# Two transformer blocks on one core: the join from the last convolved down product to the pooling mixer and the next feed-forward, rearranged by token halves

## The chip, the cores and the metric

The kernel runs on one NeuronCore of a Trainium2 chip. The metric is the device time of one execution, in microseconds (us). All five engines of the core are used: TensorE (PE, matrix products into PSUM), VectorE (DVE), ScalarE (ACT), GpSimd (POOL), and SyncE (SP), which issues the DMA transfers of the weights.

## The reference

Two blocks are computed one behind the other, in float32, on 512 tokens of width 1024. The change lies in the second. Its input is 16 meta tokens and 512 tokens (528 in all); its layers alternate a mixer and a convolved feed-forward:

```python
def pool_mixer(h, w_group, scale):
    hf = h.astype(jnp.float32).reshape(B, L, N_POOL_GROUPS, POOL_GROUP_DIM)
    csum = jnp.cumsum(hf, axis=1)
    for g, w in enumerate(POOL_WINDOWS):          # 2, 4, 8, 16
        cg = csum[:, :, g, :]
        prev = jnp.pad(cg[:, :L - w], ((0, 0), (w, 0), (0, 0)))
        means.append((cg - prev) / jnp.minimum(t, float(w))[None, :, None])
    mixed = (jnp.stack(means, axis=2) - hf)
    return jnp.einsum('blgc,gcd->blgd', mixed, w_group).reshape(B, L, D) * scale

def conv_ffn(h, w_up, conv_w, conv_b, w_down):
    u = conv_b + sum(conv_w[j] * up[:, j:j + L] for j in range(CONV_WIDTH))   # up = padded h @ w_up
    gate, val = jnp.split(u, 2, axis=-1)
    return (jax.nn.silu(gate) * val) @ w_down

for i in range(2):                                # mixer 0 is attention, mixer 1 is pooling
    h = h + rmsnorm(mixer_i(rmsnorm(h, norm_mix_pre[i])), norm_mix_post[i])
    f = conv_ffn(rmsnorm(h, norm_ffn_pre[i]), ...)
    h = h + rmsnorm(f, norm_ffn_post[i])
```

## The kernel before

Activations are stored transposed: a tile holds 128 channels on the partitions and the tokens along the columns, so X, the residual stream, is 8 tiles (KD = 8) of 528 columns (S2; S3 = 516 columns from the second feed-forward on, since the first tokens are no longer needed there). Every product is made exact enough by splitting both factors into a high and a low part of type fp32r: three products high*high, high*low, low*high (lines 642, 644, 646). A *unit* is one block of weights that fills a slot: its raw values come by DMA (a ring of 4), ScalarE makes the high part (`act_hi`, line 582), GpSimd the low part (`pool_unit`, line 567), TensorE uses it (`pe_unit`). 528 columns do not fit one PSUM bank, so a unit writes a *pair* of banks, PS[0] to PS[3], half of the columns in each. Each engine has its own program, written out by hand in the order in which it is to run, and semaphores join them.

The norm is put behind the product: a tile is multiplied by its gain and split (`act_split`, `dve_split`, line 745), and the product is scaled by 1/rms when it leaves PSUM. The sum of squares comes from ScalarE's squares (`act_square`, line 740) by either VectorE adding them (`dve_acc`, line 755) and one product with a matrix of ones (`pe_norm`, line 658), or by eight products with ones that add up in PSUM (`pe_square`, line 665). Then come the mean (`dve_norm`, line 794), exp(-0.5 ln) on ScalarE (lines 775, 776) and a Newton step on VectorE (`newton`, lines 780 to 782).

The stretch that is changed runs like this in the kernel before:

1. the last down product of the first convolved feed-forward (`cffn0`, 8 units of 6 row tiles, in a run-time loop), each unit over all 528 columns; VectorE adds each unit to M (line 1241), ScalarE squares it, VectorE adds the square to `acc`;
2. `pe_post`, `dve_post`, `act_post`: the norm of M, then for each of 8 tiles a scaled copy (line 1264) and the addition to X (line 1268); ScalarE splits and squares the new X; TensorE sums these squares;
3. `dve_pool`, `pe_pool`, `act_pool`: the pooling product comes before the pooling (the two commute), 4 units for 4 groups (line 2979); ScalarE takes it out of PSUM with the pool scale into `grouped` (line 2991); VectorE multiplies it by 1/rms into `pa` (line 3036), makes the window sums by doubling spans (`window_sums`, line 3037: 1, 2, 3 and 4 additions over two tiles at once), corrects the first 16 columns (line 3041) and writes the mixed tile to M (line 3043), which ScalarE squares and TensorE sums;
4. `dve_post` again, and the first unit of `cffn1` (`pe_first_unit`), its row tiles interleaved with the sums of the squares of the new X.

An earlier join, from attention to `cffn0` (`act_mla_out`, `dve_mla_out`, `pe_skewed`), already works by halves of 264 columns. The gate path's forward scans (line 1745) are VectorE's only `tensor_tensor_scan`.

## Time and profile before

| | |
|---|---|
| median of 3 runs | 2317.04 us (2314.05 to 2332.53) |
| the profiled execution | 2314.94 us, of which the span is 2313.1 us |
| TensorE busy | 2244.0 us, 97% of the span |
| VectorE, ScalarE, GpSimd busy | 48%, 38%, 43% |
| mean granted TensorE clock | 0.988 |

The profiled execution lies 2.1 us under the median of the three runs. Times in the rows are microseconds from the start of the span unless they are marked ns. "Idle before" names the time in which the engine did nothing ahead of an instruction, and whose work ended that. The granted clock is given as a share of full speed, 2.4 GHz; 0.5 is 1.2 GHz. Operations that follow each other on an engine overlap by some tenths of a microsecond, so a chain of them is read from the distance of their starts.

### The profile page before, as it was taken

Reading aid. Unit: us, or ns where it says so; the run is one execution under the profiler, and the core shown is the slowest. Engines: PE = TensorE matmul, PEld = TensorE weight load, DVE = VectorE, ACT = ScalarE, POOL = GpSimd, SP = SyncE. Lnnn points to the kernel's source line nnn. Section 1 sums busy time; section 2 is a strip of 40 time slices with the busy share of each in tenths; the row PEclk is TensorE's granted clock in tenths of the full one; section 3 lists DMA queues with packets and bytes.
Section 4 is the critical chain, followed back from the end, with each engine's and each line's share of the span. In section 5 each row is a group of like instructions: output and inputs, shape, how many; then the busy total and the mean of one; then the engine's idle time right before and its main releaser. Section 6 shows DMA issues by size and latency. Waiting matters only on the chain.

```text
span 2313.1 us, 34738 instructions
## 1 busy us (share of the span) xinstructions
PE 2244.0 (97%) x13485; PEld 1953.1 (84%) x13485; DVE 1112.8 (48%) x1639; ACT 878.9 (38%) x1674; POOL 987.1 (43%) x747
## 2 busy tenths in 40 slices
PE   8999999999999999999999999999999868999998
PEld 6888887778887788888797879999999848989897
DVE  5313235637634532232476655752625487626255
ACT  4323234432443422222454446432423344424244
POOL 3545454542472454544451124244444412444443
PEclk9999999999999999999999999999999979999999
DMA  5333333331351233333220113133332211233332
GB/s 159 91 95 96 94 91 99 87 87 46 94 162 56 82 92 99 91 97 94 85 70 26 34 38 101 38 91 92 91 92 84 72 37 56 91 101 91 92 92 73
DMA packets 336226, 194.06 MB, mean 84 GB/s; under 512 B 7357, under 2 KB 327506, under 8 KB 336098
## 3 DMA queue, kind: packets, MB, share of 16 engines
q1 hardware_dynamic: 335570, 191.13, 28.4%
q8 instruction: 85, 1.39, 0.2%
q10 hardware_dynamic: 528, 1.19, 0.2%
q14 instruction: 43, 0.35, 0.0%
HBM read 190.20 MB, written 2.10 MB: 83 GB/s over the span
## 4 chain that ended last, share of the span: by engine, by line
PE 90%; DVE 6%; ACT 2%; issue 1%; POOL 1%; DMA 0%; DVEq 0%; POOLq 0%; SPq 0%; ACTq 0%
PE PS L642 23%; PE PS L646 23%; PE PS L644 23%; PE PS L2545 2%; PE PS L2563 2%; PE PS L949 2%; PE PS L950 2%; PE PS L951 2%; PE PS L2599 1%; PE PS L2617 1%; PE PS L665 1%; PE PS L1601 1%; PE PS L1602 1%; PE PS L1603 1%; PE PS L1945 1%
## 5 line engine op out<-in xcount | busy, mean ns | idle before, releaser
L567 POOL TENSOR_TENSOR w_lo<-raw,w_hi 128x512 fp32r<-128x512 f32 (+5 forms) x711 | 944.4, 1351 | 1270.7 <-ACT w_hi L582 1270.6
L582 ACT ACTIVATE w_hi<-raw 128x512 fp32r<-128x512 f32 (+5 forms) x711 | 395.9, 605 | 790.9 <-PE PS L646 682.2
L642 PE MATMUL PS<-XHI,w_hi 128*128 128x264 f32 (+2 forms) x2056 | 539.0, 320 | 16.1 <-DVE XLO L745 13.8
L644 PE MATMUL PS<-XLO,w_hi 128*128 128x264 f32 (+2 forms) x2056 | 531.9, 316 | 0.0
L646 PE MATMUL PS<-XHI,w_lo 128*128 128x264 f32 (+2 forms) x2056 | 530.8, 316 | 0.0
L642 PEld LDWEIGHTS PS<-XHI,w_hi 128*128 128x128 f32 x2056 | 340.4, 189 | 49.7 <-issue 18.2
L646 PEld LDWEIGHTS PS<-XHI,w_lo 128*128 128x128 f32 x2056 | 339.8, 189 | 25.2
L644 PEld LDWEIGHTS PS<-XLO,w_hi 128*128 128x128 f32 x2056 | 339.4, 189 | 25.6 <-issue 1.0
L642 PE MATMUL PS<-h_hi,w_hi 128*128 128x512 f32 (+1 forms) x704 | 210.1, 339 | 1.7 <-DVE h_lo L1218 1.6
L644 PE MATMUL PS<-h_lo,w_hi 128*128 128x512 f32 (+1 forms) x704 | 210.4, 340 | 0.0
L646 PE MATMUL PS<-h_hi,w_lo 128*128 128x512 f32 (+1 forms) x704 | 210.3, 339 | 0.0
L1185 DVE TENSOR_TENSOR u_buf<-PS,rn 128x512 f32<-128x512 f32 (+2 forms) x88 | 61.3, 696 | 233.4 <-PE PS L646 233.4
L646 PE MATMUL PS<-x_hi,w_lo 128*128 128x512 f32 x352 | 139.4, 396 | 0.0
L644 PE MATMUL PS<-x_lo,w_hi 128*128 128x512 f32 x352 | 139.2, 395 | 0.0
L642 PE MATMUL PS<-x_hi,w_hi 128*128 128x512 f32 x352 | 139.1, 395 | 0.0
L642 PEld LDWEIGHTS PS<-h_hi,w_hi 128*128 128x128 f32 x704 | 120.9, 188 | 18.6 <-DVE h_lo L1218 1.6
L646 PEld LDWEIGHTS PS<-h_hi,w_lo 128*128 128x128 f32 x704 | 120.8, 188 | 15.2
L644 PEld LDWEIGHTS PS<-h_lo,w_hi 128*128 128x128 f32 x704 | 120.4, 188 | 15.4
L1121 ACT ACTIVATE h_hi<-hid 128x512 fp32r<-128x512 f32 (+5 forms) x88 | 56.0, 637 | 200.7 <-DVE hid L1216 200.5
L1185 DVE TENSOR_TENSOR g_buf<-PS,rn 128x512 f32<-128x512 f32 (+2 forms) x88 | 61.0, 693 | 97.1 <-PE PS L646 96.9
L1237 DVE SCALAR_TENSOR_TENSOR X<-PS,X 128x512 f32<-128x512 f32 x48 | 33.2, 691 | 148.5 <-PE PS L646 148.5
L1218 DVE TENSOR_TENSOR h_lo<-hid,h_hi 128x512 f32 (+5 forms) x88 | 69.6, 790 | 72.3 <-ACT h_hi L1121 72.3
(409 smaller groups left out, 3382.9 us busy)
## 6 DMA issues: line engine op xcount, KB each, us to landing
raw<-in_ffn_w_up SPq DMA_DIRECT2D x132, 512.0 KB, 3.8
raw<-in_ffn_w_down SPq DMA_DIRECT2D x70, 512.0 KB, 3.8
raw<-in_ffn_w_gate SPq DMA_DIRECT2D x44, 512.0 KB, 3.8
raw<-in_w_in SPq DMA_DIRECT2D x25, 512.0 KB, 3.8
raw<-in_ffn_w_down SPq DMA_DIRECT2D x24, 384.0 KB, 3.4
raw<-in_xattn_w_kv SPq DMA_DIRECT2D x16, 512.0 KB, 3.9
raw<-in_w_out SPq DMA_DIRECT2D x8, 512.0 KB, 3.9
raw<-in_xattn_w_q SPq DMA_DIRECT2D x8, 512.0 KB, 4.1
```

The lines of the kernel that those rows point to most:

```text
L567: ins = nc.gpsimd.tensor_tensor(d, r, h.bitcast(F32), ALU.subtract)
L582: ins = nc.scalar.activation(d, r, ACT.Copy)
L642: nc.tensor.matmul(ps, wh, ahi(k)[:, c:c + w], start=(k == 0), stop=False)
L644: nc.tensor.matmul(ps, wh, alo(k)[:, c:c + w], start=False, stop=False)
L646: ins = nc.tensor.matmul(ps, wl, ahi(k)[:, c:c + w], start=False, stop=(k == u.kt - 1))
L949: nc.tensor.matmul(ps, h_hi[:, k, ts], s_hi[:, cs], start=start, stop=False)
L950: nc.tensor.matmul(ps, h_hi[:, k, ts], s_lo[:, cs], start=False, stop=False)
L951: return nc.tensor.matmul(ps, h_lo[:, k, ts], s_hi[:, cs], start=False, stop=stop)
L1121: nc.scalar.activation(h_hi[:, a + 2 * it, 0:w], hid[:, 0:w], ACT.Copy).then_inc(hid_hi, 1)
L1185: nc.vector.tensor_tensor(sv(dst, blk), psv(m % 4, blk), r, ALU.mult).then_inc(unit_read, 1)
L1218: nc.vector.tensor_tensor(h_lo[:, a + 2 * it, 0:w], hid[:, 0:w], h_hi[:, a + 2 * it, 0:w].bitcast(F32), ALU.subtract).then_inc(hid_lo, 1)
L2545: ins = nc.tensor.matmul(bank[:, 0:CW], w, x[:, k, c * CW:(c + 1) * CW], start=st, stop=sp_)
```

## The change

All of it lies between the last down product of `cffn0` and the first up products of `cffn1`.

- The columns are cut in two halves, QA (270 tokens) and QB (258). The last down product runs its 8 units over QA first, then over QB. It is no longer a run-time loop. The first three units leave their last row tile for later, and 5 of 6 row tiles of unit 0 over QB run before it. Seven of the eight units' weights are held in slots of their own (`dx`, `dc`), since they are used twice; the eighth and the first two pool units use the usual slots.
- Norm, addition to X and split of half QA run on VectorE and ScalarE while TensorE works on QB of the down product. The pooling product also goes by halves: 8 products over QA, then 8 over QB, through six PSUM banks. Squares of the new X go to eight places for QA (in `ws`, `sq`) and five for QB, so that they need not wait for TensorE's sums.
- Pooling itself keeps the full width: `pa` is filled by halves (two tiles in one instruction), and the window sums of groups 1 to 3 are now two `tensor_tensor_scan` instructions per group (a running sum that adds the newest column and subtracts the one that leaves the window); group 0 keeps one addition.
- The low parts of the first two units of `cffn1` are made by VectorE (`dve_low`), not by GpSimd; these two and the next two have slots of their own.
- Behind the pooling sums TensorE issues 44 products of the identity with itself (`SPARE`), whose result nobody reads.
- The first two units of `cffn1` are summed together, row tile by row tile (`pe_join_up`), the squares of the new X go to four places, and a tile's low part is issued one step earlier than before (in iteration k for tile k - 2, was k - 3). The first up stage of `cffn1` is written out as that of `cffn0` is.

```diff
@@ -311,6 +318,13 @@
     M_tok = flat(M)[:, 0:NT * D].rearrange("p (t d) -> p t d", t=NT)
     e_hi, e_lo = ([flat(t)[:, i * SLOT:(i + 1) * SLOT] for i in range(2)] for t in (XHI, XLO))
     gain_row = flat(sq)[:, 0:D]
+    QA, QB = slice(0, QW[0]), slice(QW[0], S2)
+    SQM = [flat(sq)[:, i * QW[0]:(i + 1) * QW[0]] for i in range(2)]
+    ws_row = ws[:, :, :, :].rearrange("p a b s -> p (a b s)")
+    SQA = [ws_row[:, i * QW[0]:(i + 1) * QW[0]] for i in range(KD - 1)] + [SQM[0]]
+    SQC = [ws_row[:, i * S3:(i + 1) * S3] for i in range(4)]
+    SQB = [flat(sq)[:, 2 * QW[0]:2 * QW[0] + QW[1]], flat(sq)[:, 2 * QW[0] + QW[1]:2 * S2], acc[:, 0:QW[1]],
+           acc[:, QW[1]:2 * QW[1]], fin_rn[:, 0:QW[1]]]
 
     PS = [ctx.enter_context(nc.psum_tensor(f"PS{i}", [P, 2, 512], F32)) for i in range(4)]
 
...
+    N_DOWN, N_POOL, N_CF1 = PHASE["pool"] - KD, PHASE["pool"], PHASE["cffn1"]
+    held_of = lambda t, at: (t[:, at, 0, :], t[:, at, 1, :])
+    HELD.update({N_DOWN + i: held_of(dx, i) for i in range(5)})
+    HELD.update({N_DOWN + 5 + i: held_of(dc, i) for i in range(2)})
+    HELD.update({N_POOL + i: (w_hi[:, N_POOL % SPLIT, i * 512:(i + 1) * 512], w_lo[:, N_POOL % SPLIT, i * 512:(i + 1) * 512])
+                 for i in range(2)})
+    HELD.update({N_POOL + 2: held_of(dc, 1), N_POOL + 3: held_of(dc, 0)})
+    HELD.update({N_CF1 + i: (flat(x2_hi)[:, i * SLOT:(i + 1) * SLOT], flat(x2_lo)[:, i * SLOT:(i + 1) * SLOT])
+                 for i in range(4)})
+    assert (N_DOWN + 7) % SPLIT == (N_CF1 + 5) % SPLIT != N_POOL % SPLIT == (N_CF1 + 4) % SPLIT
+
...
+        def half(j, c, ks=None, ready=None):
+            return pe_unit(pe, n + j, 0, FLAT[n + j], lambda k: h_hi[:, k, :], lambda k: h_lo[:, k, :],
+                           [(bank(down_pair(j), c), QA.stop * c, QW[c])], ready, signal=False, wait=False, ks=ks)
...
+        for j in range(3):
+            pe.wait_ge(unit_read, n + j - 3)
+            half(j, 0, range(nt - 1), (lambda k: pe.wait_ge(hid_lo, h0 + k + 1)) if j == 0 else None)
+        half(0, 1, range(nt - 1))
+        pe.wait_ge(hid_lo, h0 + nt)
+        for j in range(3):
+            pe_q.inc(half(j, 0, range(nt - 1, nt)), ("a", j))
+        for j in range(3, KD):
+            if j == 3:
+                pe.wait_ge(unit_read, n)
+            else:
+                dve_q.wait(pe, ("ma", j - 4))
+            pe_q.inc(half(j, 0), ("a", j))
+        half(0, 1, range(nt - 1, nt)).then_inc(unit_summed, 1)
+        for j in range(1, KD):
+            if j >= 4:
+                pe.wait_ge(unit_read, n + j - 3)
+            half(j, 1, ready=sum_a if j == 1 else None).then_inc(unit_summed, 1)
+
...
+            product_a(m)
+        for k in range(6):
+            square_a(k)
+        pe.wait_ge(unit_read, N_DOWN + 7)
+        for g in range(3):
+            product_b(2 * g)
+            product_b(2 * g + 1)
+            square_b(2 * g)
+            square_b(2 * g + 1)
+            if g < 2:
+                square_a(6 + g)
+        square_b(6)
+        product_b(6)
+        square_b(7)
+        product_b(7)
+        evicted(pe, 14)
+        for k in ALL:
+            pe_square(pe, S_POOLP, 3, 2, k)
+        for _ in range(SPARE):
+            nc.tensor.matmul(PS[0][:, 1, 0:P], ident, ident, start=True, stop=True)
+
+    def pe_join_up(pe, n):
+
+        def part(j, ks):
+            return pe_unit(pe, n + j, 0, FLAT[n + j], lambda k: hi(k, 3), lambda k: lo(k, 3), outs_of((n + j) % 4, 3),
+                           signal=ks[-1] == KD - 1, wait=False, ks=ks)
+
         pe.wait_ge(unit_read, n)
-        for k in range(KD):
-            pe_square(pe, S_POOL, SUMS, 2, k)
-        for g in range(4):
-            pe.wait_ge(lo_done, 2 * (n + g + 1))
-            s = (n + g) % SPLIT
-            pe.wait_ge(x_lo, KD * D_POOL + 2 * g + 2)
-            for mt in range(2):
-                m = 2 * g + mt
-                if m >= 3:
-                    pool_out(pe, m - 3)
-                for k in range(2):
-                    c0 = k * 256 + mt * P
-                    wh, wl = w_hi[:, s, c0:c0 + P], w_lo[:, s, c0:c0 + P]
-                    for w, x, st, sp_ in ((wh, hi, k == 0, False), (wh, lo, False, False), (wl, hi, False, k == 1)):
-                        for ps, c, cw in outs_of(m % 3, 2):
-                            ins = nc.tensor.matmul(ps, w, x(2 * g + k, 2)[:, c:c + cw], start=st, stop=sp_)
-            ins.then_inc(unit_summed, 1)
-        pe.wait_ge(norm_ms, S_POOL + 1)
-        for m in range(KD):
-            pe_square(pe, S_POOLP, SUMS, 2, m)
...
+        square_a(3)
+        square_a(4)
+        post_b(2)
+        square_a(5)
+        evict(6)
+        post_b(3)
+        evict(7)
+        square_a(6)
+        post_b(4)
+        square_a(7)
+        post_b(5)
+        evict(8)
+        evict(9)
+        post_b(6)
+        evict(10)
+        evict(11)
+        post_b(7)
+        dve_q.wait(act, "mspa")
+        act_q.inc(act_rsqrt(act, sd[:, QA], ms[:, QA]), "sdpa")
+        act.wait_ge(norm_ms, S_POOL + 1)
+        act_rsqrt(act, sd[:, QB], ms[:, QB]).then_inc(norm_sd, 1)
+        evict(12)
+        evict(13)
+        evict(14)
+        evict(15)
+        for k in ALL:
+            dve_q.wait(act, ("xm", k))
+            act_square(act, S_POOLP, k, k, M[:, k, :], S2)
+            if k in (1, 3):
+                hi_at(N_CF1 + k // 2)
+        act_sqrt(act, S_POOLP, S2)
+
...
+        def pooled(g, win):
+            tiles, sums = (2 * g, 2 * g + 1), ws[:, g % 2]
+            if g == 0:
+                link(nc.vector.tensor_tensor(sums, pa[:, 0:2, 16:], pa[:, 0:2, 15:S2 + 15], ALU.add))
+            else:
+                for i, k in enumerate(tiles):
+                    link(nc.vector.tensor_tensor_scan(sums[:, i, :], pa[:, k, 16:], pa[:, k, 16 - win:S2 + 16 - win], 0.0,
+                                                      ALU.add, ALU.subtract))
             cor = const[:, C_COR + 16 * g:C_COR + 16 * (g + 1)]
             for i in range(2):
-                link(nc.vector.tensor_tensor(src[:, i, 16:32], src[:, i, 16:32], cor, ALU.mult))
+                link(nc.vector.tensor_tensor(sums[:, i, 0:16], sums[:, i, 0:16], cor, ALU.mult))
             for i, k in enumerate(tiles):
-                pool_mixed.inc(nc.vector.scalar_tensor_tensor(M[:, k, :], src[:, i, 16:], 1.0 / win, pa[:, k, 16:], ALU.mult,
-                                                              ALU.subtract), k)
-        pool_mixed.wait(dve, KD - 1)
+                dve_q.inc(nc.vector.scalar_tensor_tensor(M[:, k, :], sums[:, i, :], 1.0 / win, pa[:, k, 16:], ALU.mult,
...
+        link(nc.vector.memset(pa[:, :, 0:16], 0.0))
+        dve.wait_ge(norm_sd, S_CF0P + 1)
+        root(QB)
+        for k in range(KD + 2):
+            post_b(1, k, QB, G_FPOST[0], low_b)
+            if k == 8:
+                pe_q.wait(dve, ("sx", KD - 1))
+                dve_q.inc(mean(QA, bank(1, 0)), "mspa")
+        dve.wait_ge(acc_done, KD * (S_POOL + 1))
+        mean(QB, bank(1, 1)).then_inc(norm_ms, 1)
+        act_q.wait(dve, "sdpa")
+        root(QA)
+        for g in range(4):
+            normed(g, 0)
+        dve.wait_ge(norm_sd, S_POOL + 1)
+        root(QB)
+        for g, win in enumerate(WINDOWS):
+            normed(g, 1)
+            pooled(g, win)
+        dve.wait_ge(lo_done, 2 * N_CF1)
+        dve_low(dve, N_CF1, 0)
+        dve_low(dve, N_CF1, 1)
+        dve.wait_ge(acc_done, KD * (S_POOLP + 1))
+        nc.vector.tensor_scalar(two(ms[:, 0:S2]), psv(3, 2), 1.0 / D, EPS, ALU.mult, ALU.add).then_inc(norm_ms, 1)
+        dve_low(dve, N_CF1 + 1, 0)
+        dve_low(dve, N_CF1 + 1, 1)
+        dve.wait_ge(norm_sd, S_POOLP + 1)
+        root(slice(0, S2))
+        for k in range(KD + 2):
+            post_b(2, k, slice(0, S2), G_POST[1], lambda m: dve_split(dve, D_CF1, m, 3, G_FPRE[1]))
+        dve_norm(dve, link, S_CF1, (N_CF1 + 3) % 4, 3)
 
 
```

The halves' bodies on VectorE (`post_a`: scale, low part of the tile before, addition to X; `acc_a`, `acc_b`: add a square; `normed`: below) stand in this order in `dve_join`:

```diff
+        def normed(g, c):
+            q, at = (QA, QB)[c], 16 + c * QW[0]
+            for m in (2 * g, 2 * g + 1):
+                evicted(dve, c * KD + m)
+            link(nc.vector.tensor_tensor(pa[:, 2 * g:2 * g + 2, at:at + QW[c]], M[:, 2 * g:2 * g + 2, q],
+                                         rn[:, q].rearrange("p (o w) -> p o w", o=1).to_broadcast([P, 2, QW[c]]), ALU.mult))
+
...
+        act_q.wait(dve, "sda")
+        root(QA)
+        add_half(1, 1)
+        add_half(2, 1)
+        acc_b(0)
+        post_a(0)
+        post_a(1)
+        add_half(3, 1)
+        acc_b(1)
+        post_a(2)
+        post_a(3)
+        acc_b(2)
+        add_half(4, 1)
+        post_a(4)
+        acc_b(3)
+        post_a(5)
+        add_half(5, 1)
+        post_a(6)
+        acc_b(4)
+        add_half(6, 1)
+        acc_b(5)
+        add_half(7, 1)
+        acc_b(6)
+        post_a(7)
+        post_a(8)
+        dve.wait_ge(norm_sum, len([x for x in range(S_CF0P + 1) if x not in PE_SUMMED]))
+        mean(QB, PS[0][:, 0, 0:QW[1]]).then_inc(norm_ms, 1)
```

## Rows read from the trace of the kernel before

**Rows 1.** the page: the chain that ended last, by engine
```profile
PE 90%; DVE 6%; ACT 2%; issue 1%; POOL 1%; DMA 0%; DVEq 0%; POOLq 0%; SPq 0%; ACTq 0%
```

**Rows 2.** busy us and count of each engine, granted clock, DMA share, GB/s, by stretch
```profile
1810.00:1840.20 30.20, 29.51 (x240) 29.33 (x240) 10.56 (x16) 11.06 (x22) 16.05 (x14) 1.00 0.25 73
1840.20:1862.90 22.70, 12.19 (x38) 8.46 (x39) 17.34 (x26) 12.54 (x21) 1.40 (x2) 0.70 0.11 32
...
1870.00:1900.70 30.70, 15.65 (x70) 11.92 (x68) 29.79 (x34) 9.87 (x17) 7.39 (x6) 0.73 0.24 68
1900.70:1914.60 13.90, 3.90 (x9) 2.55 (x9) 8.32 (x13) 5.17 (x9) 0.00 (x0) 0.62 0.00 1
1914.60:1919.20 4.60, 4.60 (x18) 4.19 (x19) 4.60 (x8) 1.23 (x2) 0.00 (x0) 0.58 0.02 4
```

**Rows 3.** TensorE alone: busy us and count, granted clock, DMA share, GB/s
```profile
1852.00:1857.00 5.00, 4.72 (x11) 0.50 0.00 0
1857.00:1862.00 5.00, 4.99 (x20) 1.00 0.00 0
```

**Rows 4.** who TensorE waited for, 1780 to 1960 us: total, times, longest
```profile
PE PS L665 <- ACT sq L740: 22.6, 5, 7.9
PE PS L642 <- DVE XLO L745: 9.9, 1, 9.9
...
PE PS L642 <- DVE h_lo L1218: 0.9, 1, 0.9
```

**Rows 5.** timeline of VectorE: start, us, instruction, count [idle before it]
```profile
1870.00 2.29 DVE L3036 TENSOR_TENSOR pa<-grouped,rn 128x528 f32<-128x528 f32 x2
...
1873.65 2.37 DVE L3041 TENSOR_TENSOR pb<-pb,const 128x16 f32<-128x16 f32 x2
...
1877.30 3.47 DVE L3036 TENSOR_TENSOR pa<-grouped,rn 128x528 f32<-128x528 f32 x2
...
1892.21 1.44 DVE L3036 TENSOR_TENSOR pa<-grouped,rn 128x528 f32<-128x528 f32 x2
...
1899.36 1.33 DVE L3043 SCALAR_TENSOR_TENSOR M<-pc,pa 128x528 f32<-128x528 f32 x2
1904.79 0.71 DVE L794 TENSOR_SCALAR ms<-PS 128x528 f32<-128x528 f32 x1 [4.11 <-PE PS L665]
...
1913.69 0.75 DVE L745 SCALAR_TENSOR_TENSOR XLO<-X,cols,XHI 128x516 fp32r<-128x516 f32 x1
```

**Rows 6.** timeline of TensorE at the first unit behind pooling
```profile
1914.58 0.77 PE L642 MATMUL PS<-XHI,w_hi 128*128 128x258 f32 x2 [9.90 <-DVE XLO L745]
...
1920.38 1.03 PE L665 MATMUL PS<-sq,const 128*128 128x258 f32 x4
...
1921.97 1.03 PE L665 MATMUL PS<-sq,const 128*128 128x258 f32 x4
```

**Rows 7.** timeline of VectorE in the earlier join by halves (264 columns)
```profile
1431.42 0.43 DVE L2855 TENSOR_SCALAR ms<-PS 128x264 f32<-128x264 f32 x1 [1.05 <-PE PS L2455]
...
1434.21 0.43 DVE L2874 TENSOR_TENSOR post_t<-M,rn 128x264 f32<-128x264 f32 x1
...
1440.21 0.49 DVE L2877 SCALAR_TENSOR_TENSOR XLO<-X,cols,XHI 128x264 fp32r<-128x264 f32 x1
...
1441.65 0.42 DVE L2874 TENSOR_TENSOR post_t<-M,rn 128x264 f32<-128x264 f32 x1
```

**Rows 8.** the only scans: count, ns min/median/max, first and last start
```profile
L1745 DVE TENSOR_TENSOR_SCAN t<-const,t x4: 2130/2136/2203, 426.5 to 433.1; 128x512 f32<-128x512 f32 x4
```

**Rows 9.** VectorE, 1840 to 1935 us: busy us, mean ns, idle before
```profile
L3037 DVE TENSOR_TENSOR pb<-pa 128x1086 f32<-128x1086 f32 x4 | 5.2, 1290 | 0.1
```

**Rows 10.** timeline of ScalarE in the earlier join by halves
```profile
1438.00 0.52 ACT L2727 ACTIVATE XHI<-X,cols 128x264 fp32r<-128x264 f32 x1 [0.59 <-DVE X L2881]
...
1438.74 0.37 ACT L2722 ACTIVATE sq<-PS 128x264 f32<-128x264 f32 x1
```

**Rows 11.** GpSimd, 1803 to 1842 us: busy us, mean ns, idle before
```profile
L567 POOL TENSOR_TENSOR w_lo<-raw,w_hi 128x384 fp32r<-128x384 f32 x14 | 16.6, 1209 | 16.7 <-ACT w_hi L582 16.7
```

More of the change, by code:

```diff
@@ L400, in ffn_units @@
                     segs += [Unit(1, D, lambda i, k=f0 + j: row[k]) for j in range(n)]
+                continue
+            if straight_end and f0 + n == FT:
+                segs += [Unit(n, P, lambda i, j=j, dv=dv: dv[:, :, j, :]) for j in range(KD)]
                 continue
@@ L1112, in up @@
                         ahead(n, 2 * it + a, 2 if 2 * it + a < PAIRED else 1)
[L1113 removed]
+                    elif not third:
                         look(it, n, 2 * a + 1, count)
@@ L3045, in dve_pool @@
-        pool_mixed.wait(dve, KD - 1)
+                dve_q.inc(nc.vector.scalar_tensor_tensor(M[:, k, :], sums[:, i, :], 1.0 / win, pa[:, k, 16:], ALU.mult,
+                                                         ALU.subtract), ("xm", k))
+        add_half(0, 0)
+        for j in range(1, KD):
+            add_half(j, 0)
+            acc_a(j - 1)
+        acc_a(KD - 1)
+        add_half(0, 1)
+        pe_q.wait(dve, "sa")
+        dve_q.inc(mean(QA, bank(3, 0)), "msa")
+        act_q.wait(dve, "sda")
```

420 lines of the change are left out of this document (300 added, 120 removed).

## Prediction

> **What bounds the kernel now.** The chain of waits is 90% TensorE [rows 1], so nearly everywhere only fewer or faster products would help. The exception is the join that the change rewrites. The table of stretches [rows 2] cuts it up: in the last down product (1810 to 1840) TensorE is busy for 29.5 of 30.2 us, 0.123 us for each of 240 instructions; in the norm and split behind it (1840.2 to 1862.9) for 12.2 of 22.7; in pooling (1870.0 to 1900.7) for 15.7 of 30.7, while VectorE works for 29.8; in the last norm (1900.7 to 1914.6) for 3.9 of 13.9. The waits [rows 4] name the cause: 22.6 us for squares from ScalarE, themselves late by VectorE, and 9.9 us for the first low part. So between 1840 and 1915 VectorE's chain sets the end, and it is this chain that has to be priced. From 1914.6 on TensorE is the bound again; its start there is cold: clock 0.58 over 4.6 us [rows 2], against 1.59 us for one row tile with its square later on [rows 6]. Two row tiles that would take 3.2 us took 4.9 (1914.58 to 1919.47), so at full clock the same work would have started at 1914.58 + 1.7 = 1916.3. That is the time to beat.
>
> **1. Down product by halves.** 36 instructions of 264 columns for a unit become 18 of 270 and 18 of 258, the same columns. The wait for the last hidden tile (0.9 us, [rows 4]) goes, covered by five row tiles of unit 0's second half (5 x 3 x 0.123 = 1.8 us). But the weights are now wanted every 2.2 us in the first pass, where they were wanted every 4.4. GpSimd makes a unit's low part in 2 x 1.2 us [rows 11], slower than that; the slots of their own let it start early, and I charge 0.3 us. Gain 0.6: the product ends near 1839.5. Lower bound of the gain: each of the five last units late by 2.4 - 2.2 gives 1 us more.
>
> **2. To the second half's norm.** Half QA is complete 5 x 2.2 + 8.5 us after the start at 1803.7, near 1823.4, and its sum, queued in unit 1 of QB, near 1826.2. From mean to scaled first tile the earlier join takes 2.8 us [rows 7], so VectorE has the root at 1829.0. Until the last low part of QA it issues 8 x 3 instructions for the tiles, 7 additions of QB and 7 accumulations, 38 in all. The earlier join issues 4 in 1.44 us [rows 7], 0.36 each: 13.7 us; with waits for ScalarE's high parts I take 15, near 1844. The addition to M of unit 7 stands in that queue and comes at 1842, not at 1839.5, and the sum of QB's squares behind it, whose products on TensorE stand between pooling products 1 and 2. Mean, 2.8 us, and ScalarE's copies ahead of its root (1 us): root of QB near 1848. Before it was 1848.8. So the hidden work buys less than 1 us here: it moved in front of the end and then VectorE is late with the end.
>
> **3. To the sum of the new X's squares.** VectorE needs 8 x 3 x 0.36 = 9 us more. ScalarE must issue 19 instructions until the sixth QA square, at 0.37 each (two in 0.74, [rows 10]) some 6.5 us from 1846.4: 1852.9. Behind that square TensorE's queue holds 7 pooling products over QB (6 x 0.12 = 0.72 us each), 8 sums over QB and 2 over QA. A sum over all columns costs 1.59 - 0.73 = 0.87 us [rows 6], a half 0.43: together 5.0 + 4.3 = 9.4, with handoffs 10.3. The mean is made at 1863.2. If the clock fell, this block would double (rival C). VectorE then idles 3 us, since the root of QA is queued behind this wait.
>
> **4. To the start of the window sums.** Mean 0.47, two roots of 3 x 0.47, and four instructions that scale half QA over two tiles (540 elements, as long as one of 528: 0.72 + 0.03, [rows 5], two in 1.44): 0.47 + 2.8 + 3.0 = 6.3 us, 1869.5. Before: 1870.0 [rows 5]. So up to here 0.5 us.
>
> **5. Window sums.** Removed: 10 additions over two tiles, 1.29 us each [rows 9] and 0.03 between, of which one stays in group 0: 9 x 1.32 = 11.9 us. Added: 6 scans. The only scans of the trace take 2.14 us for 512 elements [rows 8], 4.2 ns for an element, while a two-input addition over 528 takes 0.72. For 528: 2.20 + 0.03, 6 of them 13.4 us. So the scans alone cost 1.5 us. The operations differ (multiply and add there, add and subtract here), so I keep bounds: nothing saved at 2.2, and 0.73 each (a plain addition) would give 9.0 us back. I take 2.2, the row of the instruction itself. The Trainium skill (DVE: opcode table, instruction layouts, handler registers and perf-mode slots; Datapath and trigger behaviour) says that the built-in scan "runs at half throughput". By that a scan would be an estimated 1.25 us and the sum 5.9 us lower; the trace does not agree, 2.14 us is about a quarter of an element per cycle.
> Half of the scaling is done ahead (4 x 0.75 = 3.0 us, charged in step 4). And GpSimd is silent now: before, it made low parts at 1870 to 1880, and the first two pairs of scalings took 2.29 and 3.47 us where the undisturbed pair at 1892.21 took 1.44 [rows 5]. The corrections of group 0 took 2.37 us; in group 3 they are 1899.36 - 1892.21 less the pair (1.48) and four additions (5.28), so 0.39. Together 0.85 + 2.03 + 1.98 = 4.9 us of the 30.7 were this disturbance. New length: group 0 0.75 + 1.33 + 0.41 + 1.25 = 3.7; each other group 0.75 + 4.46 + 0.41 + 1.25 = 6.9; sum 24.4 against 30.7, a gain of 6.3 (4.9 + 3.0 - 1.5). The pair of mixed tiles that ends it starts at 1892.6 (before 1899.36), the mean stays 5.4 us behind, since TensorE is still at 0.5 there: 1898.0 (before 1904.79). The four low parts on VectorE (0.7 us each) fit the idle 4.1 us before this mean and the 1.4 us of ScalarE's root; without that cover they would cost 2.8.
>
> **6. The first unit.** From the mean to the first low part was 8.9 us [rows 5]; it is issued one iteration earlier, two instructions of 0.65 less (two mixed tiles in 1.33, [rows 5]): 7.6, so TensorE could start at 1898.0 + 7.6 + 0.9 = 1906.5. But the 44 spare products are queued ahead. One is two instructions of 128 columns; a 258-column one takes 0.22 us, which bounds it below at 0.107, and the 0.123 of a 264-column fp32r instruction with its weight load is what I take: 88 x 0.12 = 10.6 us (9.4 at least). TensorE starts at 1908.6, 2 us after it could, but warm: it came up within 5 us of steady work at 1852 to 1857 [rows 3], and the two last sums (3.9 us) stand in front. I add 0.3 for a cold rest. 1908.9 stands against 1916.3. Summing two units together makes TensorE's work per row tile 0.73 + 0.73 + 0.87 = 2.33 us, above VectorE's three instructions (1.95), so nothing waits; the product work is the same, its norm comes 2 us later relative to the start and is wanted only after four units (30 us). Held slots and the written-out stage repeat `cffn0`, where TensorE shows no wait.
>
> **Sum.** 0.5 (steps 1 to 4) + 6.3 (5) + 1.3 - 2.1 + 1.7 - 0.3 (6) = 7.4 us. The profiled execution took 2314.94, giving 2307.5; the median before is 2.1 above that execution, and I put half of that on: 2308.5.
>
> **Rivals.** A, scans nearer to a plain addition (bound 0.73 us): up to 9 us more, 2299 to 2304. For it: other operations than in the row. Against: the feedback is the same. B, the spare products are slow, no gain at the end: should TensorE stay at 0.5 through them, each takes twice 0.107, and all 88 x 0.215 = 18.9 us, the first unit starts at 1898.0 + 18.9 = 1916.9 and runs warm later: 2315 to 2317, no change. Against it [rows 3]: steady work raised the clock in under 5 us. C, which ends slower: TensorE's work in the join is now cut in pieces with pauses, the clock falls at about 1848 and stays low, so the 10.3 us of step 3 become 20.6 and the mean comes at 1873.5. The start of pooling slips by as much, the end is 10.3 - 7.4 = 3 us slower, 2319 to 2320. It decides once more than 7 us of step 3's work runs at 0.5. For it: 0.5 in all of pooling's fragments; against: no pause here is over 2 us, and [rows 3]. D, more is gained in steps 2 to 4 than my queue count allows (ScalarE and VectorE never wait for each other, the mean at 1860): 2305. E, the front is not won: GpSimd late with the low parts and ScalarE at its full 0.52 us for an instruction put 3 to 4 us in front of step 4: 2311 to 2313.
>
> **Numbers.** Chances: forecast 0.50, A 0.13, B 0.08, C 0.07, D 0.08, E 0.14. The range 2301 to 2316 leaves out part of A and C, and the scatter of single runs. A measurement of this kernel tells about 1%, 23 us, from no change. All cases lie inside that: same 0.93, faster 0.04 (a scan as cheap as an addition and half of the whole join hidden too), slower 0.03 (C together with waits that I don't see).
>
> **What would show it.** Scans at 2.2 us for 528 (1.25 would be the page's, 0.7 A's); VectorE's mean before pooling near 1863 and `pa` from 1869.5; no scaling over 0.8 us; pooling 24 to 25 us long; mean behind it near 1898; spare products 10 to 11 us at clock 1.0; first unit of `cffn1` near 1909, its row tiles 2.33 us apart. Wrong would be: a clock of 0.5 between 1850 and 1863, TensorE waiting for low parts in the first pass over QA, or a new wait of TensorE in `cffn1` after its fourth unit.

## The result, and the profile of the changed kernel

| | before | changed |
|---|---|---|
| median, 20 runs each | 2316.68 us (2314.05 to 2332.53) | 2304.51 us (2299.12 to 2318.62) |
| ratio to before, 95% interval | | 0.9943 [0.9929, 0.9956] |
| the profiled execution (span) | 2314.94 us (2313.1) | 2303.09 us (2301.3) |

The median fell by 12.2 us where 8.5 was forecast; it lies inside the range, and the change is faster by 0.6%. The spans can't be subtracted to the microsecond. The work ahead of the join is the same in both, yet the last down product starts at 1803.74 in one profile and at 1806.71 in the other: and over all profiles of this study it lies between 1802.75 and 1807.67. TensorE's granted clock ahead of it differs from profile to profile (between 400 and 600 us 0.99 before, 0.97 after, up to 1.00 in others), but that stretch is not the whole of it: the second profile of the changed kernel has 0.99 there too and starts at 1806.38. The cause stays open. So everything below is measured from that start, called S (a start in the profile less S):

| us after S | before | forecast | changed | changed, second profile |
|---|---|---|---|---|
| down product ends | 36.4 | 35.8 | 36.6 | 36.6 |
| pooling loop starts (first full-width `pa`) | 66.3 | 65.8 | 67.1 | 67.0 |
| last pair of mixed tiles | 95.6 | 88.9 | 84.4 | 84.4 |
| mean behind pooling | 101.1 | 94.3 | 87.9 | 89.5 |
| first unit of `cffn1` | 112.6 (warm equivalent) | 105.2 | 97.5 | 99.0 |
| end of the span | 509.4 | 502.0 | 494.6 | 496.0 |

The stretches of [rows 2] in the profile of the changed kernel (busy us and count of PE, PEld, DVE, ACT, POOL; granted clock; DMA share; GB/s). The last line is the second stretch moved by 2.96 us, the difference of the two S, so that it covers the same distances as before:

```profile
1810.00:1840.20 30.20, 30.04 (x242) 29.56 (x241) 19.80 (x43) 14.50 (x34) 15.86 (x16) 1.00 0.37 109
1840.20:1862.90 22.70, 18.72 (x125) 16.59 (x124) 19.29 (x48) 17.50 (x48) 3.04 (x4) 1.00 0.17 47
1867.60:1873.00 5.40, 0.67 (x6) 0.46 (x4) 5.13 (x10) 2.30 (x6) 0.00 (x0) 1.00 0.00 0
1873.00:1891.00 18.00, 9.79 (x24) 6.49 (x24) 17.31 (x27) 5.86 (x10) 0.00 (x0) 0.62 0.00 0
1891.00:1904.10 13.10, 11.55 (x95) 11.29 (x96) 11.78 (x19) 5.01 (x9) 0.00 (x0) 1.00 0.29 81
1904.10:1914.00 9.90, 9.84 (x68) 9.04 (x68) 9.90 (x13) 5.84 (x11) 3.62 (x2) 1.00 0.19 55
...
1843.17:1865.87 22.70, 18.72 (x119) 16.38 (x118) 17.15 (x42) 17.98 (x50) 3.04 (x4) 1.00 0.17 47
```

Behind the down product, where TensorE worked for 12.2 of 22.7 us at a clock of 0.70, it works for 18.7 at 1.00; pooling is still VectorE's (17.3 of 18.0 us); from 1904.1 on TensorE is full and warm. VectorE's timeline through pooling, against [rows 5]:

```profile
1867.60 0.43 DVE L3287 TENSOR_SCALAR ms<-PS 128x258 f32<-128x258 f32 x1 [3.05 <-PE PS L2993]
...
1869.36 2.99 DVE L3334 TENSOR_TENSOR pa<-M,rn 128x540 f32<-128x540 f32 x4
...
1873.77 0.70 DVE L3334 TENSOR_TENSOR pa<-M,rn 128x516 f32<-128x516 f32 x1
1874.50 1.26 DVE L3340 TENSOR_TENSOR ws<-pa 128x1056 f32<-128x1056 f32 x1
...
1878.18 2.55 DVE L3343 TENSOR_TENSOR_SCAN ws<-pa 128x528 f32<-128x528 f32 x2
1880.76 0.39 DVE L3347 TENSOR_TENSOR ws<-ws,const 128x16 f32<-128x16 f32 x2
...
1888.12 2.55 DVE L3343 TENSOR_TENSOR_SCAN ws<-pa 128x528 f32<-128x528 f32 x2
...
1891.12 1.33 DVE L3349 SCALAR_TENSOR_TENSOR M<-ws,pa 128x528 f32<-128x528 f32 x2
...
1894.64 0.71 DVE L3410 TENSOR_SCALAR ms<-PS 128x528 f32<-128x528 f32 x1 [0.99 <-PE PS L717]
```

The scans are the surprise: two in 2.55 us, where step 5 charged 4.46. The group of the six in the same profile (min, median and max ns):

```profile
L3343 DVE TENSOR_TENSOR_SCAN ws<-pa x6: 1257/1257/1257, 1878.2 to 1889.4; 128x528 f32<-128x528 f32 x6
```

TensorE behind pooling, and who it waited for between 1780 and 1960 us (against [rows 4] and [rows 6]):

```profile
1892.55 2.05 PE L717 MATMUL PS<-sq,const 128*128 128x264 f32 x8 [2.92 <-ACT sq L778]
1894.44 9.99 PE L3098 MATMUL PS<-const 128*128 128x128 f32 x88
1904.18 0.49 PE L694 MATMUL PS<-XHI,x_hi 128*128 128x258 f32 x2
...
1911.36 0.59 PE L694 MATMUL PS<-XHI,x_hi 128*128 128x258 f32 x2
...
1913.71 0.47 PE L694 MATMUL PS<-XHI,x_hi 128*128 128x258 f32 x1
```

```profile
PE PS L717 <- ACT sq L778: 14.5, 4, 9.5
...
PE PS L694 <- DVE h_lo L1258: 0.2, 1, 0.2
```

The 88 spare instructions take 1904.18 - 1894.44 = 9.74 us, 0.111 us each; the wait of 9.9 us for the first low part is gone; row tiles start 2.2 to 2.7 us apart, four steps in 9.53 us (2.38 each, forecast 2.33); the wait for the last hidden tile fell from 0.9 to 0.2 us.

### The profile page after: what moved, and what is told of

Same layout as the page of the kernel before. It is cut to its first block, busy times and chain, and to the rows that moved or that the text cites. A ratio compares the mean times of both kernels' runs of the same rounds, so it can differ in the third digit from the quotient of the medians.

```text
span 2301.3 us, 34925 instructions
## 1 busy us (share of the span) xinstructions
PE 2250.9 (98%) x13575; PEld 1961.4 (85%) x13575; DVE 1116.5 (49%) x1687; ACT 883.9 (38%) x1710; POOL 984.8 (43%) x743
## 4 chain that ended last, share of the span: by engine, by line
PE 89%; DVE 7%; ACT 2%; issue 1%; POOL 1%; DMA 0%; DVEq 0%; POOLq 0%; SPq 0%; ACTq 0%
PE PS L694 23%; PE PS L698 23%; PE PS L696 23%; PE PS L2558 2%; PE PS L2576 2%; PE PS L987 2%; PE PS L988 2%; PE PS L989 2%; PE PS L2612 1%; PE PS L2630 1%; PE PS L1614 1%; PE PS L1615 1%; PE PS L1616 1%; PE PS L1958 1%; PE PS L1976 1%
## 5 line engine op out<-in xcount | busy, mean ns | idle before, releaser
L618 POOL TENSOR_TENSOR w_lo<-raw,w_hi 128x512 fp32r<-128x512 f32 (+4 forms) x685 | 915.6, 1359 | 1173.1 <-ACT w_hi L634 1173.0
L634 ACT ACTIVATE w_hi<-raw 128x512 fp32r<-128x512 f32 (+4 forms) x685 | 383.3, 608 | 779.0 <-PE PS L698 674.9
L694 PE MATMUL PS<-XHI,w_hi 128*128 128x264 f32 (+2 forms) x1992 | 525.3, 320 | 6.2 <-DVE XLO L783 3.9
L696 PE MATMUL PS<-XLO,w_hi 128*128 128x264 f32 (+2 forms) x1992 | 520.0, 318 | 0.0
L694 PE MATMUL PS<-h_hi,w_hi 128*128 128x512 f32 (+2 forms) x620 | 194.1, 346 | 0.8 <-DVE h_lo L1258 0.7
L696 PE MATMUL PS<-h_lo,w_hi 128*128 128x512 f32 (+2 forms) x620 | 194.6, 347 | 0.0
L698 PE MATMUL PS<-h_hi,w_lo 128*128 128x512 f32 (+2 forms) x620 | 194.1, 347 | 0.0
L694 PEld LDWEIGHTS PS<-h_hi,w_hi 128*128 128x128 f32 x620 | 108.2, 188 | 17.6 <-DVE h_lo L1258 1.6
L698 PEld LDWEIGHTS PS<-h_hi,w_lo 128*128 128x128 f32 x620 | 108.2, 188 | 15.2
L696 PEld LDWEIGHTS PS<-h_lo,w_hi 128*128 128x128 f32 x620 | 107.9, 188 | 15.5
```

The lines of the kernel that those rows point to most:

```text
L618: ins = nc.gpsimd.tensor_tensor(d, r, h.bitcast(F32), ALU.subtract)
L634: ins = nc.scalar.activation(d, r, ACT.Copy)
L694: nc.tensor.matmul(ps, wh, ahi(k)[:, c:c + w], start=(k == 0), stop=False)
L696: nc.tensor.matmul(ps, wh, alo(k)[:, c:c + w], start=False, stop=False)
L698: ins = nc.tensor.matmul(ps, wl, ahi(k)[:, c:c + w], start=False, stop=(k == u.kt - 1))
```

## The experiments

What each run measured, in the same distances (us after S), each from one profile. The number behind a label is that of the experiment, and "run 4" below is the experiment numbered 4; runs 3 and 6 were executed once, so they have no median:

| | loop starts | last mixed pair | mean behind | first unit | end |
|---|---|---|---|---|---|
| before | 66.26 | 95.62 | 101.05 | 110.84 (cold) | 509.36 |
| changed | 67.06 | 84.41 | 87.93 | 97.47 | 494.59 |
| e1_adds (1) | 66.99 | 88.48 | 93.85 | 103.62 | 500.45 |
| e2_before_scans (2) | 66.24 | 91.48 | 95.08 | 104.87 | 503.93 |
| e3_scan_mult (3) | 67.06 | 84.41 | 88.61 | 99.13 | 495.86 |
| e4_no_spare (5) | 67.03 | 84.37 | 87.90 | 96.51 (cold) | 495.42 |
| e5_pool_low (4) | 67.03 | 87.90 | 91.42 | 100.96 | 498.04 |
| e6_late_dx (6) | 66.62 | 83.98 | 87.50 | 97.04 | 494.04 |
| v3_root_first (7) | 64.54 | 81.89 | 85.41 | 94.95 | 491.97 |
| v2_all_small (8) | 64.58 | 81.93 | 85.45 | 94.07 | 491.01 |
| v4_best (9) | 64.11 | 81.45 | 86.05 | 94.70 | 491.58 |
| after_again (10) | 67.04 | 84.38 | 89.47 | 99.01 | 496.02 |

**1. The scans undone in the changed kernel.** The window sums by doubling again, the rest as changed:

```diff
-    ws = sb("ws", [P, 2, 2, S2], scope=pool_scope)
+    ws = sb("ws", [P, 2, 2, S2 + 16], scope=pool_scope)
...
-                    link(nc.vector.tensor_tensor_scan(sums[:, i, :], pa[:, k, 16:], pa[:, k, 16 - win:S2 + 16 - win], 0.0,
-                                                      ALU.add, ALU.subtract))
...
+            src, span, turn = pa[:, 2 * g:2 * g + 2, :], 1, 0
+            while span < win:
+                to, lo_ = ws[:, turn], 2 * span - 1
+                link(nc.vector.tensor_tensor(to[:, :, lo_:], src[:, :, lo_:], src[:, :, lo_ - span:S2 + 16 - span], ALU.add))
+                src, span, turn = to, 2 * span, 1 - turn
+            sums = src[:, :, 16:]
```

> The changed kernel with the scans of groups 1 to 3 undone: 9 additions over two tiles by doubling spans, as before, into a slightly wider ws. Theory (the cheap scans bought 4 us themselves, and their shorter gaps a warm TensorE in the pooling sums): pooling, from the first scaling of half QB to the last pair of mixed tiles, is 9 x 1.32 - 6 x 1.29 = 4.1 us longer than in the changed kernel (21.4 against 17.35), TensorE's clock is back at 0.5 behind the last pair, and from that pair to the mean it takes 5.4 us, not 3.5: 6.0 us slower than the changed kernel in the trace. Rival (the clock has nothing to do with the length of the gaps, the halves or the missing early sums did it): 4.1 us, and 3.5 us to the mean.

Measured: the loop 4.1 us longer (88.48 - 66.99 = 21.49 against 17.35), the end 5.9 later; 2311.26 us, ratio to before 0.9969 [0.9937, 1.0001]. The sum of step 5 with the scan at its true price is 9 x 1.32 - 6 x 1.29 = 4.1 us: the arithmetic was sound, its price was not. The other 1.8 us of the 5.9 lie behind the loop, in the last sums of squares (5.37 us from mixed pair to mean, 3.52 in the changed kernel); run 10 shows what they can be.

**2. The scans alone in the kernel before.**

```diff
-            src = window_sums(lambda to, a, b: link(nc.vector.tensor_tensor(to, a, b, ALU.add)), pa[:, 2 * g:2 * g + 2, :],
-                              (pb, pc), win)
+            src = (pb, pc)[g % 2]
+            if g == 0:
+                link(nc.vector.tensor_tensor(src[:, :, 16:], pa[:, 0:2, 16:], pa[:, 0:2, 15:S2 + 15], ALU.add))
+            else:
+                for i, k in enumerate(tiles):
+                    link(nc.vector.tensor_tensor_scan(src[:, i, 16:], pa[:, k, 16:], pa[:, k, 16 - win:S2 + 16 - win], 0.0,
+                                                      ALU.add, ALU.subtract))
```

> The kernel before with one thing of the change: scans in place of the additions of groups 1 to 3. Theory (1.28 us for a scan): the window sums take 4.1 us less, the time from the last pair of mixed tiles to the mean falls from 5.4 to about 3.5 if TensorE comes up to full clock in the shorter gaps: 2309 us, 4 to 6 us less than before, and the rest of the gain (9 to 11 us) belongs to the halves, the spare products and the quiet GpSimd. Rival (scans and everything else interact, the cheap scan is slower beside GpSimd's low parts): under 3 us.

Measured: the last mixed pair 4.1 us earlier, the end 5.4; 2313.63 us, ratio 0.9983 [0.9957, 1.0009]. From both sides the scans give the same 4.1 us in the loop; the forecast had them cost 1.5. The medians of runs 1 and 2 do not show it by themselves: both intervals reach past 1.

**3. Other operations in the scans.** Multiply and add, as in the gate scans of [rows 8], in place of add and subtract. The window sums are then other numbers; nothing else differs.

```diff
-                                                      ALU.add, ALU.subtract))
+                                                      ALU.mult, ALU.add))
```

> The changed kernel with the operations of the six pooling scans made multiply and add, as in the gate path, in place of add and subtract; the window sums are wrong by this, their number and size are the same. Theory (the price of a scan hangs on its operations): 2.2 us each instead of 1.28, pooling 5.6 us longer. Rival (the gate path's scans are dear by their operands or their place, a scan has one price): 1.28 us each.

```profile
1877.81 2.55 DVE L3343 TENSOR_TENSOR_SCAN ws<-pa 128x528 f32<-128x528 f32 x2
```

2.55 us for two with either pair of operations. Whatever made the gate scans 2.14 us long, it was not what they compute. This expectation fell.

**4. GpSimd at work beside the scans.** In the kernel before, GpSimd made low parts all through the gate scans (timelines of GpSimd and VectorE of the kernel before, at 424 us):

```profile
424.33 9.79 POOL L567 TENSOR_TENSOR w_lo<-raw,w_hi 128x512 fp32r<-128x512 f32 x4 [1.39 <-ACT w_hi L582]
```

```profile
426.49 8.71 DVE L1745 TENSOR_TENSOR_SCAN t<-const,t 128x512 f32<-128x512 f32 x4
```

Beside the scans a low part took 2.08 to 2.21 us there (the first of the four, beside another long instruction of VectorE, 3.28), and the two just ahead, at 420.41, took 2.54 together. So the low parts of `cffn1`'s first two units were given back to GpSimd, where they fall beside the scans of groups 1 and 2:

```diff
-        if static(it) and n in (N_CF1, N_CF1 + 1):
-            return
...
-        dve.wait_ge(lo_done, 2 * N_CF1)
-        dve_low(dve, N_CF1, 0)
-        dve_low(dve, N_CF1, 1)
...
-        dve_low(dve, N_CF1 + 1, 0)
-        dve_low(dve, N_CF1 + 1, 1)
```

> The changed kernel with the low parts of the first two cffn1 units made by GpSimd again, so that they run while VectorE is in the scans of groups 1 and 2. The scan with multiply and add cost 1.28 us in the pooling, so its operations are not what made the gate path's scans last 2.14 us; there GpSimd ran four low parts in 9.8 us beside them. Theory (a scan and a GpSimd operation that meet exclude each other, a scan alone costs 1.28): two to four of the six scans are stretched to about 2.1 us, GpSimd's low parts from 1.27 to over 2 us, pooling 2 to 4 us longer and the kernel slower by that, less nothing on VectorE behind pooling. Rival (a scan does not meet GpSimd; the gate path's are dear by their operand from the constants): scans at 1.28 us, kernel the same within 1 us.

VectorE, its scans and corrections by themselves (min, median and max ns), then GpSimd, of this run:

```profile
1875.19 3.44 DVE L3341 TENSOR_TENSOR_SCAN ws<-pa 128x528 f32<-128x528 f32 x2
1878.66 1.26 DVE L3345 TENSOR_TENSOR ws<-ws,const 128x16 f32<-128x16 f32 x2
...
1888.66 2.55 DVE L3341 TENSOR_TENSOR_SCAN ws<-pa 128x528 f32<-128x528 f32 x2
```

```profile
L3341 DVE TENSOR_TENSOR_SCAN ws<-pa x6: 1257/1257/2145, 1875.2 to 1889.9; 128x528 f32<-128x528 f32 x6
L3345 DVE TENSOR_TENSOR ws<-ws,const x8: 174/174/1053, 1872.8 to 1891.4; 128x16 f32<-128x16 f32 x8
```

```profile
1875.83 3.86 POOL L616 TENSOR_TENSOR x_lo<-raw,x_hi 128x512 fp32r<-128x512 f32 x2 [26.95 <-ACT x_hi L632]
```

The same scans take 3.44 us for two beside GpSimd and 2.55 in group 3, where GpSimd is silent; two corrections of 16 columns take 1.26 instead of 0.38. 2 x (0.89 + 0.88) = 3.5 us is just what the loop grew by (87.90 - 84.37). Only one instruction of each pair is disturbed: a scan takes 2.145 us and its neighbour 1.257, a correction 1.053 and its neighbour 0.174. The disturbed scan is as long as the gate scans' 2.14 [rows 8], though it reads other operands and computes something else. The gate scans start 2.2 us apart, each beside one low part; one behind the other the two would take 1.26 + 1.29 = 2.55 (an estimate from the undisturbed rows), so most of each instruction stands apart from the other engine's, and some tenths still overlap. The Trainium skill (SBUF — State Buffer; SBUF: two separate sides) says that VectorE, in an instruction with two inputs in SBUF, and a GpSimd instruction that reads SBUF exclude each other for a whole instruction; these rows agree, but for those tenths. The median, 2305.41 us, can't tell 3.5 us (ratio 0.9945 [0.9920, 0.9970]).

**5. No spare products.**

```diff
-    SPARE = 44
+    SPARE = 0
```

> The changed kernel without the 44 spare products. Theory (they keep TensorE warm but hold it 1.2 us past the first low part, and VectorE's third low part is late anyway): TensorE starts the first unit of cffn1 1.1 us earlier at clock 0.5, stays there for about 4.6 us, loses 2.3 us of work and gets part of it back from the earlier start: 1 to 2 us slower than the changed kernel. Rival (the spare products are a pure delay): 1 us faster. Second rival (without them the clock stays low for all of the first units): 5 us or more slower.

```profile
1899.69 0.77 PE L694 MATMUL PS<-XHI,x_hi 128*128 128x258 f32 x2 [8.65 <-DVE XLO L783]
...
1903.76 0.90 PE L694 MATMUL PS<-XHI,x_hi 128*128 128x258 f32 x2
```

```profile
1896.00:1900.00 4.00, 0.31 (x1) 0.50 0.04 13
1900.00:1904.00 4.00, 4.00 (x17) 0.50 0.02 4
1904.00:1908.00 4.00, 4.00 (x29) 0.95 0.45 131
```

The first unit starts 8.6 us behind the mean instead of 9.5, and the next row tile follows 4.07 us later (2.2 to 2.35 when warm). The end lies 0.8 us later than with the spare products: they put the first unit 1.0 us back (97.47 - 96.51) and buy 1.8 behind it, 0.8 net, where 1 to 2 was expected. 2301.52 us in the median, ratio 0.9930 [0.9905, 0.9955]: no measured median shows the spare products to be of use, and one profile a side leaves their sign open too.

**6. The high part of one down unit later.** In the changed kernel GpSimd makes six low parts without a pause from 1806.82 on (7.29 us), and VectorE's low part of the last hidden tile takes 1.55 us in their shadow. Here ScalarE makes the high part of the fourth unit only behind the last hidden tile, so that GpSimd is done earlier:

```diff
                         act_hi(act, N_DOWN + 2, 0, FLAT[N_DOWN + 2])
-                        act_hi(act, N_DOWN + 3, 0, FLAT[N_DOWN + 3])
...
+                    if n + 4 * count == N_DOWN and static(it) and it == count - 1 and a == 1:
+                        act_hi(act, N_DOWN + 3, 0, FLAT[N_DOWN + 3])
```

> The changed kernel with the high part of the fourth down unit moved behind the last hidden tile's, so that GpSimd's third low part in a row does not meet VectorE's last three operations ahead of the down product (in the changed kernel 1.31 and 1.55 us where they took 0.71 before). Theory (GpSimd beside VectorE ate the 0.6 us that the halves should have brought there): last h_lo 0.7 us long, the TensorE wait of about 0.5 us ahead of it gone, down product ends 35.8 to 36.0 us after its start (changed kernel: 36.3). Rival (the weights of the fourth unit are now what is late): 0.5 to 1 us more, 36.8 or over.

```profile
1812.38 0.71 DVE L1259 TENSOR_TENSOR h_lo<-hid,h_hi 128x528 f32 x1 [0.85 <-ACT h_hi L1158]
```

0.71 us instead of 1.55, TensorE's wait for it is gone, and the down product ends at 36.17 instead of 36.60. The 0.43 us stay to the loop and to the first unit.

**7. The root of QB and half of the scaling ahead of the wait.** Step 3 foresaw that VectorE idles 3 us before the mean of QB, with the root of QA queued behind it. The order is turned:

```diff
-        dve.wait_ge(acc_done, KD * (S_POOL + 1))
-        mean(QB, bank(1, 1)).then_inc(norm_ms, 1)
         act_q.wait(dve, "sdpa")
         root(QA)
-        for g in range(4):
-            normed(g, 0)
+        normed(0, 0)
+        normed(1, 0)
+        dve.wait_ge(acc_done, KD * (S_POOL + 1))
+        mean(QB, bank(1, 1)).then_inc(norm_ms, 1)
+        normed(2, 0)
+        normed(3, 0)
```

> The changed kernel with VectorE's queue reordered ahead of the pooling: the root of half QA and the scaling of groups 0 and 1 before the wait for the sum of QB's squares, instead of behind it. Theory (VectorE idles 3.05 us in that wait, and 2 x 0.75 of scaling can cover ScalarE's root): the window sums start 2.9 us earlier after the start of the down product, 64.2 us instead of 67.1, and everything behind follows: 2.5 to 3 us faster than the changed kernel. Rival (ScalarE's evictions 12 to 15, queued behind its root, or the cold clock in the pooling sums give it back): under 1 us at the first unit of cffn1.

```profile
1865.83 1.48 DVE L3334 TENSOR_TENSOR pa<-M,rn 128x540 f32<-128x540 f32 x2
1867.34 0.43 DVE L3287 TENSOR_SCALAR ms<-PS 128x258 f32<-128x258 f32 x1
...
1870.57 0.70 DVE L3334 TENSOR_TENSOR pa<-M,rn 128x516 f32<-128x516 f32 x1
```

No idle time stands before the mean any more; the loop starts 2.5 us earlier and the end comes 2.6 us earlier. The median is 2304.54 us (ratio 0.9937 [0.9912, 0.9961]): a gain of 2.6 us that the chain shows and the median of ten runs does not.

**8. The same with 66 spare instructions** (`SPARE = 33`), and ScalarE's high parts of units 2 and 3 of `cffn1` made later in its splits of the new X, behind tiles 4 and 6:

```diff
-            if k in (1, 5):
-                hi_at(N_CF1 + 2 + k // 4)
+            if k in (4, 6):
+                hi_at(N_CF1 + k // 2)
```

> As v3_root_first, with 33 spare products instead of 44 and the high parts of cffn1's units 2 and 3 in iterations 4 and 6 of the next post stage, not 1 and 5 (GpSimd's low part stretched two of VectorE's operations to 1.8 us there, just ahead of the third low part). Theory: first unit of cffn1 8.5 us behind the mean, not 9.5, no pause ahead of its third row tile, in all 1.2 to 1.5 us below v3_root_first, 4 us below the changed kernel. Rival (the stretch only moves into later row tiles, where TensorE then waits; or unit 2's weights are late): the same as v3_root_first within 0.3 us, with a wait of TensorE for a low part.

The first unit starts 0.9 us earlier than in run 7, the end comes 1.0 earlier, a little less than the 1.2 expected: the pause ahead of the third row tile is gone, but one of 0.3 us now stands ahead of the sixth, where VectorE's two instructions of 1.8 us have moved, so its rival held in part. 2305.22 us in the median, ratio 0.9938 [0.9916, 0.9960].

**9. All of it together**, the edits of 6, 7 and 8:

> This kernel joins the three edits that each gained something from S, the start of the last down product: root of QB and half of the scaling ahead of the waited-for mean (-2.5 us at the window sums), 66 spare products instead of 88 with the high parts of units 2 and 3 of cffn1 later (-1.0 at the first unit), ScalarE's high part of the last down unit later (-0.4 at the end of the down product). Theory (each lies on the chain that sets the end, so they add): window sums start 64.1 us after S, mean of cffn1's sum at 111.2, end at 490.6, which is 4.0 us less than the changed kernel's 494.6. Rival (the 0.4 us ahead of the join is swallowed, because the sums before pooling wait for ScalarE and not for TensorE): window sums at 64.5 and end at 491.0. Against the kernel before, from S: 18.8 us less, ratio near 0.992.

**10. The changed kernel again**, without an edit, on the same chip as 9:

> The changed kernel once more, unedited, beside the combined version on one chip. Theory: the end lies 494.6 us after S within 0.5, as in its first profile, whatever S is; the combined version's median lies some 4 us (0.17%) under this one's. Rival (the distance from S scatters as much as the whole span does, and the differences of 1 to 4 us read from single profiles mean nothing): the end lies more than 1 us away from 494.6.

The combined version's median is 2301.31 us (ratio 0.9950 [0.9933, 0.9967]), the changed kernel's 2303.52 (0.9953 [0.9936, 0.9970]). Up to the loop the edits add as expected: it starts at 64.11, 2.9 us earlier than the unedited kernel's. The medians differ by 2.2 us, and the intervals lie over each other, so the combined version is not shown to be faster. The end is 491.58 against a forecast of 490.6; its mean comes 4.60 us behind the last mixed pair, 1.1 more than in runs 7 and 8.

The unedited kernel says why. Its loop starts and ends where it did (67.04 and 84.38, before 67.06 and 84.41), but its mean comes 5.09 us behind the last mixed pair instead of 3.52, and the end is 1.4 us later: this expectation fell, and the end lies where its rival put it, more than 1 us away. TensorE in the second profile:

```profile
1892.20 3.61 PE L717 MATMUL PS<-sq,const 128*128 128x264 f32 x8 [2.36 <-ACT sq L778]
1895.65 9.99 PE L3098 MATMUL PS<-const 128*128 128x128 f32 x88
1905.39 0.49 PE L694 MATMUL PS<-XHI,x_hi 128*128 128x258 f32 x2
```

Its granted clock, over the stretch that holds these sums of squares:

```profile
1892.00:1894.00 2.00, 1.80 (x4) 0.50 0.03 8
```

And the same stretch in the first profile:

```profile
1892.00:1894.00 2.00, 1.45 (x7) 1.00 0.00 0
```

The same eight sums take 3.61 us, for the most part at 1.2 GHz, and 2.05 at 2.4. In pooling's fragments the clock rises and falls: the four groups of eight sums took 3.86, 3.89, 2.05 and 2.05 us in the first profile and 3.86, 2.05, 2.61 and 3.61 in the second. Which level meets the last sums changes from one execution to the next of one kernel. So the 1.8 us behind the loop in runs 1 and 2 need be no property of the scans, though both kernels that add by doubling show the long distance (5.43 and 5.37) in their one profile; more profiles of them would tell. Ends of kernels whose mean lies at different distances from the last mixed pair can't be compared to better than 1.6 us. From S to that pair the two profiles agree within 0.03 us. The runs whose distance is 3.52 or 3.53 (changed kernel, 4 to 8) met the same clock there and can be compared.

## Why the forecast held, and where its terms were wrong

The time lies in the stated range, but measured from S the gain at the end is 14.8 us where 7.4 was forecast, twice as much. Nearly all waits and overlaps came as described; one price, the scan's, was wrong by 5.6 us, and the range was wide enough to hold that.

The terms, from the forecast's 7.4 us to what the profile gives at the first unit, 112.6 - 97.5 = 15.1 us: 7.4 - 1.3 + 5.75 + 1.9 + 1.3 = 15.05.

**Step 1, missed by 0.8 us.** The wait for the last hidden tile shrank, from 0.9 to 0.2, but the product ended at 36.6 instead of 35.8, no earlier than before. About half of the miss, 0.43, belongs to what is left of that wait: the six low parts in a row stretched VectorE's chain to the tile. Run 6 shows it and takes the 0.43 back. The sum charged GpSimd's time as lateness of weights and forgot what it does to VectorE. The other half, 0.45, is the sum of QA's squares, which the step moved into the down product without charging TensorE for it: from 1829.29 to 1829.98 two steps of TensorE's starts take 0.69 us instead of 0.24.

```profile
1829.29 0.28 PE L698 MATMUL PS<-h_hi,dx 128*128 128x258 f32 x1
1829.41 0.62 PE L3005 MATMUL PS<-acc,const 128*128 128x270 f32 x2
1829.66 0.48 PE L694 MATMUL PS<-h_hi,dx 128*128 128x258 f32 x1
1829.98 0.28 PE L696 MATMUL PS<-h_lo,dx 128*128 128x258 f32 x1
```

**Steps 2 to 4, missed by another 0.5 us.** The clock stayed at 1.00, so rival C did not come, and no pause over 1.3 us shows from the down product to the mean of QB. The means came at 60.9 instead of 59.5, the loop at 67.06 instead of 65.8. The mean of QB is the late one; from it to the loop the 6.2 us are the forecast's 6.3. It was late because VectorE had the root of step 2, for the second half's norm, at 45.5 instead of 44.3. The mean ahead of that root came at 41.5, 1.0 later than the step's terms put it, and the 3.8 us from there to the root became 4.0, though two of the root's three instructions took 0.84 us, where the first took 0.43, beside GpSimd's low parts of a pool unit:

```profile
1849.96 0.43 DVE L818 TENSOR_TENSOR post_t<-post_t 128x258 f32<-128x258 f32 x1 [1.21 <-ACT post_t L814]
...
1850.24 1.61 POOL L618 TENSOR_TENSOR dc<-raw,dc 128x256 fp32r<-128x256 f32 x2 [0.69 <-ACT dc L634]
...
1850.42 0.84 DVE L819 SCALAR_TENSOR_TENSOR post_t<-post_t,ms 128x258 f32<-128x258 f32 x1
```

That is 0.8 us that look like the disturbance of run 4; no run moved those low parts away. The 3 us of VectorE's idle time before it were foreseen too, and run 7 shows that they could be had.

**Step 5, the term that failed.** "I take 2.2, the row of the instruction itself": it measured 1.26 to 1.28, the six scans take 3 x (4.46 - 2.58) = 5.6 us less than charged. The estimate that the forecast worked out from the Trainium skill (DVE: opcode table, instruction layouts, handler registers and perf-mode slots; Datapath and trigger behaviour) and set aside, 1.25 us, was right: the trace gives 1.257. The row was true and was misread: it stood beside GpSimd's low parts (run 4), and the same step priced just that disturbance out of the scalings and corrections of the loop. The rest of the step held: the pairs of mixed tiles are 1.33, the corrections 0.38, the scaling 0.70. From its start to the last pair the loop takes 17.35 us where 23.1 were forecast, so the scans are all but 0.1 us of the error. The result lies between the forecast and rival A (scans at 0.73, 9.0 us), nearer to A, which got too small a chance for a row whose surroundings had not been looked at.

**Behind the loop, by chance.** The forecast kept 5.4 us from the last pair to the mean, since TensorE had been at 0.5 there. (It had not been at 0.5 in all of pooling, as rival C says: before, the first eight sums took 2.02 us, at full clock.) The first profile shows 3.52, the second 5.09 (run 10): 1.9 us gained in one, 0.3 in the other. The term is no fixed property of the kernel.

**Step 6, missed by 1.3 us.** The spare products measured 0.111 us each, not 0.12 (0.8 us of 88), and no cold rest or sum was left behind the mean (0.5). The mechanism was right, a warm start in place of a cold one at 0.58, and rival B did not come. The forecast priced the spare products as a delay of 2.1 us that buys 1.7, a net loss; run 5 has a delay of 1.0 that buys 1.8, a net gain of 0.8 us that is less than a median tells. From the first unit on nothing new waits, as said: 97.5 to 115.2, the mean of `cffn1`'s sum, with a pause of 0.4 us where GpSimd's first two low parts (3.62 us together, from 1904.21) made two of VectorE's instructions 1.80 us long.

**Against the medians** the gain is 12.2 us here and 11.1 in the second comparison (2314.58 and 2303.52), less than the 14.8 and 13.3 from S. Without the 1.9 us of the clock the terms give 7.4 - 1.3 + 5.75 + 1.3 = 13.2. The intervals of the two comparisons reach from 10.2 to 16.4 and from 6.9 to 14.8 us, so both hold it, and neither tells it from 12.
